# Stick-breaking attention in a hybrid layer: the newest softplus ahead of the older sum on VectorE

## The reference

```python
def block(args):
    qb, t0 = args
    z = jnp.einsum('bqhd,bkhd->bhqk', qb, k).astype(jnp.float32) * scale
    q_idx = t0 + jnp.arange(Q_BLOCK)
    strict = key_idx[None, :] < q_idx[:, None]
    log_1mb = jnp.where(strict, jax.nn.log_sigmoid(-z), 0.0)
    between = lax.cumsum(log_1mb, axis=3, reverse=True) - log_1mb
    w = jnp.where(strict, jnp.exp(jax.nn.log_sigmoid(z) + between), 0.0)
    return jnp.einsum('bhqk,bkhd->bqhd', w.astype(v.dtype), v)
```

## Time and profile before

| what | us |
|---|---|
| median of 3 runs | 2257.64 |
| lowest and highest of them | 2249.7 and 2270.64 |
| the profiled execution's own time | 2278.93 |
| its span | 2277.1 |
| PE busy over the span | 1945.0 (85%) |
| DVE busy | 1344.2 (59%) |
| ACT busy | 1090.5 (48%) |
| POOL busy | 549.1 (24%) |

### The profile page before, as it was taken

One profiled execution on the slowest core, in us unless ns is written; L12 is line 12 of the kernel. 1 busy time (PEld: TensorE's weight loads), 2 busy tenths in 40 slices (PEclk: granted clock), 3 DMA queues, 4 the chain that ended last, 5 costly groups with the idle time before them and its releaser, 6 DMA issues.

```text
span 2277.1 us, 35044 instructions
## 1 busy us (share of the span) xinstructions
PE 1945.0 (85%) x11552; PEld 1635.0 (72%) x11552; DVE 1344.2 (59%) x2803; ACT 1090.5 (48%) x2406; POOL 549.1 (24%) x436
## 2 busy tenths in 40 slices
PE   2399999889999999999999689998588888858887
PEld 1299999777777877777777577766366666647776
DVE  4530488657677676767676624333588888843443
ACT  4321111156566666657575523333587777831211
POOL 0000000034344443434343300011244434410000
PEclk9999999889899999989898879999699988979999
DMA  3232212200000000000001112133704030023443
GB/s 118 79 83 64 60 64 70 96 6 6 23 23 7 23 5 23 7 21 7 23 5 24 42 47 73 57 121 112 148 15 88 15 79 17 6 87 115 148 147 111
DMA packets 121825, 128.88 MB, mean 57 GB/s; under 512 B 81936, under 2 KB 94992, under 8 KB 120464
## 3 DMA queue, kind: packets, MB, share of 16 engines
q1 hardware_dynamic: 121744, 127.86, 19.3%
HBM read 85.89 MB, written 41.94 MB: 56 GB/s over the span
## 4 chain that ended last, share of the span: by engine, by line
PE 61%; DVE 17%; issue 8%; ACT 7%; DMA 5%; SPq 1%; POOL 1%; DVEq 0%; ACTq 0%; POOLq 0%
PE ps L604 6%; PE ps L558 5%; PE ps L560 5%; PE ps L559 5%; PE ps L545 5%; PE ps L546 5%; PE ps L547 5%; PE ps L590 4%; DVE small L1446 4%; PE ps L781 3%; DMA gb<-gate_scr 3%; PE ps L739 2%; PE ps L578 2%; PE ps L579 2%; PE ps L765 2%
## 5 line engine op out<-in xcount | busy, mean ns | idle before, releaser
L1591 POOL TENSOR_TENSOR ring_r<-ring,sp_hi 128x512 fp32r<-128x512 f32 (+1 forms) x320 | 358.2, 1119 | 926.1 <-DVE sp_hi L1309 926.1
L604 PEld LDWEIGHTS ps<-v,ring 128*128 128x128 f32 x2176 | 303.8, 202 | 37.4 <-issue 13.4
L604 PE MATMUL ps<-v,ring 128*128 128x65 f32 x2176 | 299.9, 280 | 5.2 <-ACT ring L960 3.3
L948 ACT ACTIVATE ring<-ps 128x512 f32<-128x512 f32 (+1 forms) x320 | 170.5, 533 | 256.2 <-PE ps L579 194.9
L545 PE MATMUL ps<-w_hl,ht_hi 128*128 128x256 f32 x896 | 253.2, 283 | 2.6 <-DVE ht_lo L1230 2.3
L546 PE MATMUL ps<-w_hl,ht_hi 128*128 128x256 f32 x896 | 252.8, 282 | 0.0
L547 PE MATMUL ps<-w_hl,ht_lo 128*128 128x256 f32 x896 | 252.7, 282 | 0.0
L1610 POOL TENSOR_TENSOR p<-p 128x1024 f32<-128x1024 f32 (+4 forms) x96 | 170.0, 1782 | 254.3 <-ACT p L1095 254.3
L558 PE MATMUL ps<-ht_hi,w_hl 128*128 128x512 f32 x448 | 200.9, 448 | 29.7 <-DVE ring L1403 9.3
L1306 DVE SCALAR_TENSOR_TENSOR ring<-ring,ps 128x512 f32<-128x512 f32 (+1 forms) x320 | 192.0, 600 | 30.5 <-ACT ring L953 29.3
L1446 DVE TENSOR_REDUCE small<-ps 128x1 f32<-128x1024 f32 (+4 forms) x192 | 168.9, 906 | 54.8 <-PE ps L739 30.4
(11 more groups left out here) (177 smaller groups left out, 3821.1 us busy)
## 6 DMA issues: line engine op xcount, KB each, us to landing
w_raw<-in_w_narrow SPq DMA_DIRECT2D x18, 512.0 KB, 3.8
xb<-in_x SPq DMA_DIRECT2D x16, 512.0 KB, 3.5
gate_scr<-ring SPq DMA_DIRECT2D x64, 128.0 KB, 1.9
w_raw<-rot_scr SPq DMA_DIRECT2D x32, 256.0 KB, 3.7
qk_scr<-w_hl SPq DMA_DIRECT2D x32, 256.0 KB, 3.4
yb<-y_scr SPq DMA_DIRECT2D x16, 512.0 KB, 5.7
gb<-gate_scr SPq DMA_DIRECT2D x16, 512.0 KB, 6.5
xr<-in_x SPq DMA_DIRECT2D x16, 512.0 KB, 5.3
```

The costliest lines, as they stand in the source:

```text
L604: mm = pe.matmul(ps[:, 4 + i % 2, j * (HD + 1):(j + 1) * (HD + 1)], ring[:, 4 + i % 2, j * P:(j + 1) * P], v1[:, kb, :], start=True, stop= ...
L1591: nc.gpsimd.tensor_tensor(ring_r[:, i % 4, j0 * P:], ring[:, i % 4, j0 * P:], sp_hi[:, i % 4, j0 * P:].bitcast(F32), ALU.subtract).then_in ...
```

## The change

In every slot of the loop DVE now issues the softplus of step i-1 (1306, 1309) ahead of the sum of step i-5 (1323, 1326 or 1320). The woven-in work stays behind both. The instructions of the other engines, and their order, are the same; DVE has the same instructions in another order.

```diff
             def sb_slot(h, i, more):
+                if 1 <= i and (more or i <= N_ST):
+                    sb_softplus(h, i - 1)
                 if i >= 5:
                     sb_add(h, i - 5)
-                if 1 <= i and (more or i <= N_ST):
-                    sb_softplus(h, i - 1)
                 for ahead, n, at in SB_PROJECT:
                     if at + 5 <= i < at + 7 and (more or not ahead):
                         sb_stack_lo(h, ahead * NT + n, i - at - 5)
                 if SB_SPLIT < i <= SB_SPLIT + DC:
                     split_lo(h + (C_SB + 1), NARROW, i - SB_SPLIT - 1)
```

## The result

| | before | changed |
|---|---|---|
| median of the runs, us | 2263.66 (4 runs) | 2295.18 (4 runs) |
| lowest and highest | 2249.7, 2270.64 | 2289.18, 2297.8 |
| profiled execution | 2278.93 | 2297.8 |
| ratio, 95% interval | | 1.0143 (1.0085 to 1.0202) |
| the same, run again: median | 2262.44 (17 runs) | 2292.03 (6 runs) |

The change costs 1.4%, some 30 us.

What follows compares the result with a forecast made beforehand. PE was taken to bound the loop, busy 761 of 827 us. Waits of 23.2 us plus 13.6 us of clock falls made 36.8 us, giving 2294.4 us on the median, with 2266 to 2322 as the range for 8 in 10.

Steps and rivals of the forecast that it cites:

- the waits: In the loop, PE's added waits from copy slots and slots 21 to 28: 23.2 us slower.
- the clock: Steps around slots 26 and 27: PE's clock falls in half of the heads, 4 x 3.4 = 13.6 us.
- What is gained: At line 590 the softplus comes earlier, but PE then waits at 604 for the later sum: nothing gained.
- Rival 1: At line 590 PE's waits for POOL go, 27 us or half: 2231 or 2244 us; chance 0.04.
- The copy slots: Late sum delays copies 1333 and 1336 or PE's values: 1.6 + 3.2 + 2.1 us before slot 12, slots 41/44, 33/34.
- Slots 21 to 28: POOL's subtraction holds line 1187: 1.7 us in seven heads, 4.4 in the last, 16.3 us together.
- rival 2: Whole loop: nearly all hides, line 1187 is not held; 8.5 us slower, 2266 us, chance 0.16.
- I take nothing: At lines 590 and 604: one wait is swapped for the other, so no gain is counted.
- its working for slot 28: PE's values of slot 28 wait for slot 27's sum, behind holds and the 1.06 us softplus pair: 1.7 us.
- The signs named in advance: In the loop's profile: 1187 about 1.0 us, 590 waits under 10, 604 waits 20 or more, clock below 0.92.

Runs made afterwards that it cites:

- the third experiment: Changed kernel with line 1187 directly behind the softplus pair and, in the copy slots only, the sum ahead of the softplus again: 2287.1 us, ratio 1.0075.
- the first experiment: Changed kernel with line 1187 back directly behind the cast, ahead of the sum: 2279.75 us, ratio 1.0076.
- the first version: Kernel before, with both copies of a tile (1333 and 1336) together in the first of their two slots: 2235.92 us, ratio 0.9889.

## Why the prediction was right, step by step

The forecast was 36.8 us slower. The medians moved by 31.5 and, with more runs, by 29.6. The absolute figures meet more closely, 2294.4 forecast and 2295.18 measured, and that is luck: the first median of the kernel before, 2257.64, was 6.0 us below the one with the fourth run, which makes up for the 5.3 us too many. Of the two parts of the sum the waits were forecast too low (23.2, measured 26.3) and the clock too high (13.6, measured 1.7 and 5.6 net).

**What is gained: nothing.** Right, and for the reason given. The waits at 590 went (31.4 to 4.4) and came back at 604. Rival 1 did not come about, since its condition failed: the values matmuls do wait for the sum, 57.5 us in all.

**The copy slots: 6.9 us.** Measured 1.9 + 4.0 + 2.9 = 8.8 (0.24 for 0.2, 0.57 for 0.45, 0.41 for 0.3 per head). The third experiment took the two latter away by putting the sum ahead again.

**Slots 21 to 28: 16.3 us.** Measured 17.5: 1.86 per head for 1.7, and 4.46 in the last head for 4.4. The lengthening of DVE's slots was worked out from one meeting behind the loop, and it is confirmed in every slot. The forecast was 0.61, 0.33, 0.06, 0, 0.61, 0.75, 0.87 and 1.01 us; in the head shown above line 1187 is longer by 0.61, 0.34, 0.08, 0, 0.63, 0.75, 0.89 and 1.03. What was wrong is where PE loses the time, and how it splits. The working had PE run undelayed up to one wait in slot 28. The profile has no wait in slot 28 of the first seven heads, but waits for the sum of 0.70, 0.58, 0.71, 0.54, 0.41 and 0.89 us in slots 20 to 23, 26 and 27. And rival 2, without the holds, left only 0.2 us per head here, where the first experiment shows 0.87 and the third, with the copy slots restored as well, 0.62. The step that failed is "I take nothing", carried too far: the late sum was taken to cost no more than the waits at 590 that it replaces. In slot 26, where PE's step took only 1.13 us before, a late sum adds 0.93 us, of which the next step gives 0.45 back. The term still came out near its size because its working for slot 28 had both in it, the holds and the 1.06 us; since the waits stand elsewhere, some of that is luck.

Accordingly rival 2 was priced too low: 8.5 us, where the kernel without holds is 15.7 us above before by the medians (17 by its ratio, 1.0076).

**The clock: 13.6 us.** Falls in steps 18 to 30 in four of eight heads were taken at 3.4 us each. In the first seven heads they came in two and three, at 3.8 us each on average (of five), so 7.7 and 11.3 us; a short one in the last head is no longer in the time to step 37. The size of one was about right, their number too high. Two more steps of this term failed. It took the falls around slots 4 and 12 as unchanged, but they cost 6.0 and 5.7 us less, so that the clock's net part is 1.7 and 5.6 us. And it reasoned from the waits ahead of slots 26 and 27, while the falls began in slots 21 to 23. Its reading of the earlier trace rows has a flaw too: the 6 us from 878 already hold part of the fall (0.74 in their second half), so they are not only what PE did before it.

**The signs named in advance.** Line 1187 median 0.894 us, forecast 1.0 (five of the eight per head take 0.89 to 1.32, as named); waits at 590 under 10 (4.4); waits at 604 57.5 (20 or more); mean clock 0.91; the loop 850 us where 860 had been said. The wait of 578 before slot 12 was to read 2.7 and reads 1.9, since 0.79 of it is booked on 604 in slot 11.

What stays open: why the clock falls in one head and not in the next. The places shift when the waits shift (the third experiment and the first version), and no run here pins down the rule.

## What to carry to other kernels

An instruction that fills the time between a handover and the other engine's start is free only in that place: before a reordering, look up which engine begins what behind each instruction, and whether the two can hold each other up. Here that was GpSimd's subtraction of two SBUF operands against VectorE's subtraction of two SBUF operands, or its cast out of SBUF. If a consumer waits for two results of one engine, moving one ahead of the other swaps the wait; the order pays only where the one that is now late has slack. And a saving is to be measured between fixed points of the program, for a total of waits can stay the same while time goes.

## What the runs showed of the hardware that was not expected

The falls of TensorE's clock behave like something that is pushed about. With the wait before slot 12 shortened from 2.46 to 0.89 us, the fall behind it went in seven of eight heads (13.03 to 13.15 us in steps 13 to 18, from 14.4 to 15.9), and falls turned up in steps 18 to 30, which they had not touched, in six heads of the first profile and three of the second. Runs of one and the same kernel differ by it: those of the third experiment range over 42 us, with mean clocks from 0.925 down to 0.905, so here a comparison of two or three runs can't carry a difference of 10 us.

VectorE's copy with its input in PSUM and output in SBUF (line 1320) was not held by POOL. In the kernel before, 23 of the loop's 32 copies began while POOL subtracted, and every one took 0.42 or 0.43 us, as the others did:

```profile
949.32 0.42 DVE L1320 COPY acc<-ps 128x256 f32<-128x256 f32 x1
```
```profile
949.31 1.30 POOL L1591 TENSOR_TENSOR ring_r<-ring,sp_hi 128x512 fp32r<-128x512 f32 x1 [0.46 <-DVE sp_hi L1309]
```

The cast of line 1309 was held. In the changed kernel, behind the short copy of a tile's first step:

```profile
962.12 0.68 DVE L1306 SCALAR_TENSOR_TENSOR ring<-ring,ps 128x512 f32<-128x512 f32 x1
962.83 0.80 DVE L1309 CAST sp_hi<-ring 128x512 fp32r<-128x512 f32 x1
```
```profile
962.05 1.30 POOL L1591 TENSOR_TENSOR ring_r<-ring,sp_hi 128x512 fp32r<-128x512 f32 x1 [1.38 <-DVE sp_hi L1309]
```

POOL ended at 963.35, and the cast, which takes 0.43 us alone, took 0.80 and ended at 963.63. Six heads have such a cast, of 0.79 to 0.81 us, and each ends 0.28 us behind POOL. So the cast of an SBUF operand meets POOL as well. The Trainium skill has this too ("SBUF — State Buffer", section "Who interferes with whom"): copies and casts can run in a mode that takes the port shared with GpSimd, if their operands meet certain conditions. The rows agree: from PSUM not held (0.42 us), from SBUF held (0.80 us). The kernel before had it too, in smaller measure: the loop's longest cast outside its first steps went from 0.575 to 0.805 us with the change.
